# A state-space kernel's phase tables on GpSimd: two tables per instruction up to the last doubling

## The chip, the cores and the metric

One core of one Trainium2 chip runs the whole program. The metric is the device time of one execution in microseconds; lower is better. Inputs and outputs are float32.

## The reference

The program computes two stacked blocks on a sequence of 256 rows of width 1024. The first block has two layers (feed-forward, mixer, cross-attention to a memory of 256 rows, feed-forward); the mixer of the first layer is called even, that of the second odd. The second block has three parallel branches, one of which is a diagonal complex state-space recurrence with 2048 states, and a last feed-forward. What the change touches is the recurrence, cut to its core:

```python
ab_re, ab_im = mag * jnp.cos(li * dt), mag * jnp.sin(li * dt)      # one complex factor per state
x_re = jnp.einsum('bsgh,gph->bsgp', uf, bb_re)                     # inputs of the states
x_im = jnp.einsum('bsgh,gph->bsgp', uf, bb_im)
# h[t] = ab * h[t-1] + x[t], by an associative scan over the 256 rows
_, _, h_re, h_im = lax.associative_scan(combine, (a_re, a_im, x_re, x_im), axis=1)
y = einsum(h_re, c_re) - einsum(h_im, c_im) + d_skip * uf
```

## The kernel before

The kernel turns the input of the states by the angle of each row, scans with the real magnitude only, and turns the result back. For that it needs, for every state, the cosine and sine of the state's angle times 1 to 256. These are the phase tables: four tables J = 0 to 3 of 128 partitions by 2 (cosine, sine) by 4 blocks by 256 rows, 1 MB each.

They are built early, on GpSimd, while the first feed-forward runs, and written ("spilled") to DRAM, from where they are read back in the second block. `phase_table(J)` (L2728) waits for the angles of VectorE, copies the 8 first columns (L2736) and then doubles: from n columns it makes columns n to 2n, by a complex product with column n-1. Each doubling is two triples: two products into the scratch `K.tabs` (L2744, L2745; `vsb` in the trace) and their difference or sum into the table (L2747; `R` in the trace). `before()` makes GpSimd wait for its own last instruction ahead of L2744 and of L2747. Eight doublings of 4n = 4 to 512 elements a partition make a table. The DMA at L2750 spills it. Tables 0 and 2 are built in `K.qT`, tables 1 and 3 in `K.kT`, two neighbouring quarters of `R1`; so table J from 2 on waits for the spill of J-2. Next on GpSimd's queue is `decay_bias` (L2759), which waits for VectorE in the even mixer. ScalarE waits for spills 2 and 3 ahead of its first write to `qT` in the even mixer (L1327, L1328).

The other engines run their own programs in a fixed order written out by hand. All weights are float32 and are split into two parts for TensorE: SyncE's queue loads a piece into `raw` (five buffers), ScalarE rounds it to `whi` (L1118), VectorE computes the rest `wlo` (L1677), and TensorE multiplies with both (L445 to L447). There are three buffers of each part: ScalarE can round a piece when TensorE has finished the one three pieces before, and VectorE works two pieces ahead of TensorE. What else VectorE has to do stands between two L1677, in program order.

One such thing is `row_rstd` (from L1715 on), the reciprocal root of the mean square of the rows of a normalisation. It is a chain of small instructions, each waiting for the one before: L1726, L1729, L1731 and L1732 (these two don't depend on each other), L1734, and three times two L1738 and two L1742. In the first feed-forward it runs for the memory's rows, `row_rstd("m")`, after the sixth chunk of columns. At the start of the even and the odd mixer it runs for the rows of `x`; behind it L1747 (VectorE) and L1144 (ScalarE) write the normalised rows `O`, which TensorE transposes (L511). The lower part of the memory's transposed rows (`mT`, L1762) is computed in eight steps between the weight pieces of the tenth and eleventh chunk of the first feed-forward.

Of the kernel before, what the change touches and what calls it, by code (L numbers as in the profile page):

```python
# [10 lines left out]
ALU = mybir.AluOpType  # L11
ACT = mybir.ActivationFunctionType
AX = mybir.AxisListType.X
P = 128
# [102 lines left out]
class Kernel:  # L117
# [33 lines left out]
    def memory(self):  # L151
# [9 lines left out]
        R1 = self.R1 = sb("R1", [P, 8192])  # L161
# [38 lines left out]
        self.CL = [b.rearrange("p (j n) -> p j n", j=4) for b in self.sqj]  # L200
        self.early = [self.qT, self.kT]
        self.pq0 = [a.rearrange("p (r j) n -> p r j n", r=2) for a in self.early]
        self.pq = [self.M[:, i, :].rearrange("p (r j n) -> p r j n", r=2, j=2) for i in range(2)]
        self.spill = self.nc.dram_tensor("phases", (4, P, 2048), F32, kind="Internal").ap()
        self.cum = self.nc.dram_tensor("cum", (8, 256), F32, kind="Internal").ap()
# [8 lines left out]
        c = self.cst  # L214
# [119 lines left out]
BLOCKS = (0, 2, 1, 3)  # L334
# [2357 lines left out]
def pool_program(K, G, A):  # L2692

    S, E, D = K.S, K.nc.gpsimd, K.D
    pool = Engine(E)

    def before():

        pool.wait_ge(*S.pool_own.latest())
# [20 lines left out]
    def mem_load():  # L2720

        pool.wait_ge(*S.turned.at("squares"))
        for t in range(2):
            E.dma_start(K.O[:, t, :], D["mem"].rearrange("b (t p) d -> t p (b d)", p=P)[t]).then_inc(*S.mem.done(0, step=16))
        pool.wait_ge(*S.xlo.at(("h", "f0", 3, 1)))
        mem_turned(0)

    def phase_table(J):  # L2728

        tab = K.pq0[J % 2]  # L2730
        pool.wait_ge(*S.trig.at("phases"))
        if J >= 2:
            pool.wait_ge(*S.spilled[J - 2].at(0))
        for ri in range(2):
            for i, block in enumerate(BLOCKS):
                E.tensor_copy(tab[:, ri, i, 0:1], K.SM[:, 2 + ri, 4 * J + block:4 * J + block + 1]).then_inc(*S.pool_own.done())  # L2736
        n = 1
        while n < 256:
            c, s = tab[:, 0, :, 0:n], tab[:, 1, :, 0:n]
            cw, sw = (tab[:, i, :, n - 1:n].to_broadcast([P, 4, n]) for i in range(2))  # L2740
            u1, u2 = K.tabs[:, 0, :, 0:n], K.tabs[:, 1, :, 0:n]
            for out, (a, b), op in ((0, (cw, sw), ALU.subtract), (1, (sw, cw), ALU.add)):
                before()
                E.tensor_tensor(u1, c, a, ALU.mult).then_inc(*S.pool_own.done())  # L2744
                E.tensor_tensor(u2, s, b, ALU.mult).then_inc(*S.pool_own.done())  # L2745
                before()
                E.tensor_tensor(tab[:, out, :, n:2 * n], u1, u2, op).then_inc(*S.pool_own.done())  # L2747
            n *= 2
        before()
        E.dma_start(K.spill[J], K.early[J % 2].rearrange("p k t -> p (k t)")).then_inc(*S.spilled[J].done(0, step=16))  # L2750

    def load_table(q):

# [5 lines left out]
    def decay_bias():  # L2759

        pool.wait_ge(*S.scan.at("neg"))
        E.dma_start(K.cum, K.cumT[:, 1, :]).then_inc(*S.cum.done(0, step=16))
        pool.wait_ge(*S.cum.at(0))
        E.dma_start(K.biasA[:, :, :], bass.AP(K.cum.tensor, K.cum.offset, [[0, P], [256, 8], [1, 256]])).then_inc(*S.dec.done(0, step=16))
# [45 lines left out]
    small_loads()  # L2810
    pool.wait_ge(*S.loaded[0].at(20))
    mem_load()
    for J in range(4):
        phase_table(J)
    decay_bias()
    for t in range(2):
        decay_rows(t, range(4))
# [68 lines left out]
def build(nc, D, known):  # L2886

    with ExitStack() as ctx:
        K = Kernel(nc, D, ctx, known)
        G, A = gemms(K), attentions(K)  # L2890
        pe_program(K, G, A)
        act_program(K, G, A)
        dve_program(K, G, A)
        pool_program(K, G, A)
        sp_program(K, G, A)
        return K.known()
# [61 lines left out]
```

## Time and profile before

| | |
|---|---|
| median of 3 runs | 1626.81 us (1624.32 to 1627.3) |
| profiled execution, its own time | 1623.05 us |
| its span (first to last instruction) | 1621.8 us |
| granted TensorE clock | 0.999 |
| TensorE matmul busy | 1595.5 us (98%) |
| VectorE busy | 1109.3 us (68%) |
| ScalarE busy | 861.6 us (53%) |
| GpSimd busy | 227.5 us (14%) |

In the profile PE is TensorE (PEld its weight loads), DVE is VectorE, ACT is ScalarE, POOL is GpSimd and SPq is SyncE's DMA queue. A row of a timeline gives the start in us from the span's start, the length in us, the engine, the line of the kernel, the instruction with what it writes and reads, and in brackets how long the engine had been idle before it and for whom. Rows that follow each other with the same line are merged, with their count (x2). The length of an instruction counts what it waits inside the engine. Matmuls overlap, so a row of 0.39 us may start 0.23 us after the one before it.

### The profile page before, as it was taken

Reading aid. Unit: us, or ns where it says so; the run is one execution under the profiler, and the core shown is the slowest. Engines: PE = TensorE matmul, PEld = TensorE weight load, DVE = VectorE, ACT = ScalarE, POOL = GpSimd, SP = SyncE. Lnnn points to the kernel's source line nnn. Section 1 sums busy time; section 2 is a strip of 40 time slices with the busy share of each in tenths; the row PEclk is TensorE's granted clock in tenths of the full one; section 3 lists DMA queues with packets and bytes.
Section 4 is the critical chain, followed back from the end, with each engine's and each line's share of the span. In section 5 each row is a group of like instructions: output and inputs, shape, how many; then the busy total and the mean of one; then the engine's idle time right before and its main releaser. Section 6 shows DMA issues by size and latency. Waiting matters only on the chain.

```text
span 1621.8 us, 21203 instructions
## 1 busy us (share of the span) xinstructions
PE 1595.5 (98%) x8050; PEld 1331.2 (82%) x8050; DVE 1109.3 (68%) x1769; ACT 861.6 (53%) x1324; POOL 227.5 (14%) x351
## 2 busy tenths in 40 slices
PE   8999999999999999999999999999999999999998
PEld 6888877788888888888889888888889877888886
DVE  6775788867655556555596775655568997776566
ACT  5554556855545445444555555544454457454444
POOL 2499901000000000000000000000014442100000
PEclk9999999999999999999999999999999999999999
DMA  9766656445455565655654553555685554556563
GB/s 283 242 208 213 207 169 191 150 142 156 140 185 188 188 186 178 191 185 190 213 171 156 163 186 111 183 187 187 189 261 166 165 157 143 182 194 193 188 188 109
DMA packets 187543, 295.22 MB, mean 182 GB/s; under 512 B 13510, under 2 KB 108144, under 8 KB 186160
## 3 DMA queue, kind: packets, MB, share of 16 engines
q1 hardware_dynamic: 183264, 275.93, 54.4%
q0 software_dynamic: 3888, 17.60, 3.4%
q8 instruction: 64, 1.05, 0.3%
q10 hardware_dynamic: 288, 0.33, 0.1%
q14 instruction: 39, 0.32, 0.1%
HBM read 288.29 MB, written 5.25 MB: 181 GB/s over the span
## 4 chain that ended last, share of the span: by engine, by line
PE 86%; DVE 8%; ACT 3%; issue 2%; POOL 1%; DMA 0%; SPq 0%; DVEq 0%; ACTq 0%
PE b L445 25%; PE b L447 24%; PE b L446 24%; PE b L667 4%; DVE wlo L1677 2%; PE b L669 2%; ACT whi L1118 1%; PE b L690 1%; PE b L920 1%; PE b L902 1%; PE b L511 1%; PE b L527 1%; PE b L611 1%; PE b L564 1%; ACT R L1207 1%
## 5 line engine op out<-in xcount | busy, mean ns | idle before, releaser
L1677 DVE TENSOR_TENSOR wlo<-raw,whi 128x1024 fp32r<-128x1024 f32 (+1 forms) x523 | 648.7, 1243 | 430.6 <-ACT whi L1118 429.2
L1118 ACT ACTIVATE whi<-raw 128x1024 fp32r<-128x1024 f32 (+1 forms) x523 | 549.8, 1053 | 554.3 <-PE b L447 518.4
L445 PE MATMUL b<-whi,hT 128*128 128x512 f32 (+1 forms) x1040 | 413.0, 397 | 9.4 <-DVE wlo L1677 8.2
L447 PE MATMUL b<-whi,hT 128*128 128x512 f32 (+1 forms) x1040 | 404.8, 389 | 0.0
L446 PE MATMUL b<-wlo,hT 128*128 128x512 f32 (+1 forms) x1040 | 404.3, 389 | 0.0
L445 PE MATMUL b<-whi,oT 128*128 128x512 f32 x672 | 265.1, 394 | 0.0
L447 PE MATMUL b<-whi,oT 128*128 128x512 f32 x672 | 262.0, 390 | 0.0
L446 PE MATMUL b<-wlo,oT 128*128 128x512 f32 x672 | 261.6, 389 | 0.0
L445 PEld LDWEIGHTS b<-whi,hT 128*128 128x128 f32 x1040 | 195.8, 188 | 54.7 <-DVE wlo L1677 10.4
L447 PEld LDWEIGHTS b<-whi,hT 128*128 128x128 f32 x1040 | 195.7, 188 | 41.6
L446 PEld LDWEIGHTS b<-wlo,hT 128*128 128x128 f32 x1040 | 196.0, 188 | 37.7
L447 PEld LDWEIGHTS b<-whi,oT 128*128 128x128 f32 x672 | 126.1, 188 | 26.9
L445 PEld LDWEIGHTS b<-whi,oT 128*128 128x128 f32 x672 | 126.2, 188 | 26.2 <-DVE R L2501 0.5
L446 PEld LDWEIGHTS b<-wlo,oT 128*128 128x128 f32 x672 | 126.3, 188 | 25.3
L667 PE MATMUL b<-hT,whi 128*128 128x512 f32 x256 | 90.8, 399 | 0.0
L1207 ACT ACTIVATE R<-R,st 128x256 f32<-128x256 f32 (+1 forms) x96 | 43.5, 455 | 73.3 <-DVE st L1861 30.5
L669 PE MATMUL b<-hT,wlo 128*128 128x256 f32 x256 | 71.9, 281 | 0.0
L2822 POOL DMA_DIRECT2D biasB<-in_rel x1 | 0.5, 527 | 490.8 <-PE b L690 490.8
L1249 ACT ACTIVATE biasA<-b,st 128x256 f32<-128x256 f32 x88 | 41.1, 474 | 44.6 <-PE b L447 41.2
L445 PE MATMUL b<-hT,whi 128*128 128x256 f32 (+1 forms) x216 | 62.2, 288 | 0.1
L446 PE MATMUL b<-hT,whi 128*128 128x256 f32 (+1 forms) x216 | 61.1, 283 | 0.0
L447 PE MATMUL b<-hT,wlo 128*128 128x256 f32 (+1 forms) x216 | 61.0, 283 | 0.0
(349 smaller groups left out, 1855.9 us busy)
## 6 DMA issues: line engine op xcount, KB each, us to landing
raw<-in_ffn_w_in SPq DMA_DIRECT2D x350, 256.0 KB, 3.2
raw<-in_ffn_w_out SPq DMA_DIRECT2D x88, 512.0 KB, 3.4
raw<-in_w_ff SPq DMA_DIRECT2D x64, 512.0 KB, 4.0
raw<-in_w_in SPq DMA_DIRECT2D x36, 512.0 KB, 3.7
raw<-in_x_w_kv SPq DMA_DIRECT2D x32, 512.0 KB, 4.1
raw<-in_even_w_in SPq DMA_DIRECT2D x24, 512.0 KB, 4.2
raw<-in_odd_w_in SPq DMA_DIRECT2D x24, 512.0 KB, 4.0
raw<-in_x_w_q SPq DMA_DIRECT2D x16, 512.0 KB, 4.1
```

Source lines behind the costliest of these rows:

```text
L445: T.matmul(out, ah, bh, start=start, stop=False, skip_group_check=skip)
L446: T.matmul(out, ah, bl, start=False, stop=False, skip_group_check=skip)
L447: return T.matmul(out, al, bh, start=False, stop=stop, skip_group_check=skip)
L511: ins = T.transpose(banks[b][:, (2 * i + t) * P:(2 * i + t + 1) * P], src[:, t, kt * P:(kt + 1) * P], ident)
L527: ins = T.transpose(banks[b][:, i * P:(i + 1) * P], K.sqj[t][:, i * P:(i + 1) * P], ident)
L564: ins = T.transpose(banks[b][:, k * P:(k + 1) * P], src[:, k * P:(k + 1) * P], ident)
L667: T.matmul(bank[:, :].rearrange("p (a t) -> p a t", a=2), hi[:, kk, cs], K.hs[:, :, kt, :], start=kt == 0, stop=False, skip_group_check=True)
L669: ins = T.matmul(bank[:, 256:512], lo[:, kk, cs], K.hT[0][:, kt, :], start=False, stop=kt == 7, skip_group_check=True)
L1118: E.activation(K.whi[j % NSPLIT][:, 0:n], K.raw[j % NRAW][:, 0:n], ACT.Copy).then_inc(*S.whi.done(j))
L1207: ins = E.activation(s3[:, h, :], s3[:, h, :], ACT.Exp, bias=nm[:, h:h + 1], accum_out=sm[h])
L1249: E.activation(s[:, 0:256], bank[:, 0:256], ACT.Silu, scale=K.stat(("y", f.name), 2)[:, t:t + 1]).then_inc(*S.silu.done((f.name, c, t)))
L1677: V.tensor_tensor(K.wlo[j % NSPLIT][:, 0:n], K.raw[j % NRAW][:, 0:n], K.whi[j % NSPLIT][:, 0:n].bitcast(F32), ALU.subtract).then_inc(*S.wl ...
```

## The change

`phase_table(J)` becomes `phase_tables(first)`, which builds tables `first` and `first + 1`. A new view `K.pq01` covers `qT` and `kT` together, with the table as an extra dimension. The copies of the first columns are made for both tables (16 of them). For n = 1 to 64 one doubling with instructions of 8n elements a partition serves both tables, with the scratch split in two halves. For n = 128 the scratch holds one table only, so the two tables are doubled one after the other, each followed by its spill. The second call waits for the spills of both tables 0 and 1 before it starts. The arithmetic of each element is the same.

```diff
--- before.py
+++ after.py
@@ -200,6 +200,7 @@
         self.CL = [b.rearrange("p (j n) -> p j n", j=4) for b in self.sqj]
         self.early = [self.qT, self.kT]
         self.pq0 = [a.rearrange("p (r j) n -> p r j n", r=2) for a in self.early]
+        self.pq01 = R1[:, 4096:8192].rearrange("p (b r j n) -> p b r j n", b=2, r=2, j=4)
         self.pq = [self.M[:, i, :].rearrange("p (r j n) -> p r j n", r=2, j=2) for i in range(2)]
         self.spill = self.nc.dram_tensor("phases", (4, P, 2048), F32, kind="Internal").ap()
         self.cum = self.nc.dram_tensor("cum", (8, 256), F32, kind="Internal").ap()
@@ -2725,29 +2726,40 @@
         pool.wait_ge(*S.xlo.at(("h", "f0", 3, 1)))
         mem_turned(0)
 
-    def phase_table(J):
-
-        tab = K.pq0[J % 2]
+    def phase_tables(first):
+
         pool.wait_ge(*S.trig.at("phases"))
-        if J >= 2:
-            pool.wait_ge(*S.spilled[J - 2].at(0))
-        for ri in range(2):
-            for i, block in enumerate(BLOCKS):
-                E.tensor_copy(tab[:, ri, i, 0:1], K.SM[:, 2 + ri, 4 * J + block:4 * J + block + 1]).then_inc(*S.pool_own.done())
+        if first:
+            for J in range(first):
+                pool.wait_ge(*S.spilled[J].at(0))
+        for J in (first, first + 1):
+            for ri in range(2):
+                for i, block in enumerate(BLOCKS):
+                    E.tensor_copy(K.pq0[J % 2][:, ri, i, 0:1],
+                                  K.SM[:, 2 + ri, 4 * J + block:4 * J + block + 1]).then_inc(*S.pool_own.done())
         n = 1
         while n < 256:
-            c, s = tab[:, 0, :, 0:n], tab[:, 1, :, 0:n]
-            cw, sw = (tab[:, i, :, n - 1:n].to_broadcast([P, 4, n]) for i in range(2))
-            u1, u2 = K.tabs[:, 0, :, 0:n], K.tabs[:, 1, :, 0:n]
-            for out, (a, b), op in ((0, (cw, sw), ALU.subtract), (1, (sw, cw), ALU.add)):
-                before()
-                E.tensor_tensor(u1, c, a, ALU.mult).then_inc(*S.pool_own.done())
-                E.tensor_tensor(u2, s, b, ALU.mult).then_inc(*S.pool_own.done())
-                before()
-                E.tensor_tensor(tab[:, out, :, n:2 * n], u1, u2, op).then_inc(*S.pool_own.done())
+            if n < 128:
+                tables, both = [K.pq01], K.tabs.rearrange("p a j (b m) -> p a b j m", b=2)
+                parts = [tuple(both[:, a, :, :, 0:n] for a in range(2))]
+            else:
+                tables = [t.unsqueeze(1) for t in K.pq0]
+                parts = [tuple(K.tabs[:, a, :, 0:n].unsqueeze(1) for a in range(2))] * 2
+            for i, (tab, (u1, u2)) in enumerate(zip(tables, parts)):
+                b = len(K.pq0) // len(tables)
+                c, s = tab[:, :, 0, :, 0:n], tab[:, :, 1, :, 0:n]
+                cw, sw = (tab[:, :, r, :, n - 1:n].to_broadcast([P, b, 4, n]) for r in range(2))
+                for out, (x, y), op in ((0, (cw, sw), ALU.subtract), (1, (sw, cw), ALU.add)):
+                    before()
+                    E.tensor_tensor(u1, c, x, ALU.mult).then_inc(*S.pool_own.done())
+                    E.tensor_tensor(u2, s, y, ALU.mult).then_inc(*S.pool_own.done())
+                    before()
+                    E.tensor_tensor(tab[:, :, out, :, n:2 * n], u1, u2, op).then_inc(*S.pool_own.done())
+                if n == 128:
+                    J = first + i
+                    before()
+                    E.dma_start(K.spill[J], K.early[J % 2].rearrange("p k t -> p (k t)")).then_inc(*S.spilled[J].done(0, step=16))
             n *= 2
-        before()
-        E.dma_start(K.spill[J], K.early[J % 2].rearrange("p k t -> p (k t)")).then_inc(*S.spilled[J].done(0, step=16))
 
     def load_table(q):
 
@@ -2810,8 +2822,8 @@
     small_loads()
     pool.wait_ge(*S.loaded[0].at(20))
     mem_load()
-    for J in range(4):
-        phase_table(J)
+    phase_tables(0)
+    phase_tables(2)
     decay_bias()
     for t in range(2):
         decay_rows(t, range(4))
```

## Rows read from the trace of the kernel before

**Rows 1.** The page: busy time of each engine
```profile
PE 1595.5 (98%) x8050; PEld 1331.2 (82%) x8050; DVE 1109.3 (68%) x1769; ACT 861.6 (53%) x1324; POOL 227.5 (14%) x351
```

**Rows 2.** A stretch; columns: length, busy time (instructions) per engine, clock, DMA
```profile
80.00:120.00 40.00, 40.00 (x183) 33.11 (x181) 28.52 (x43) 20.41 (x31) 36.83 (x64) 1.00 0.67 210
```

**Rows 3.** Timeline of TensorE at the even mixer; columns: start, length, instruction, idle before
```profile
205.68 0.39 PE L447 MATMUL b<-whi,mT 128*128 128x512 f32 x1
208.29 1.38 PE L511 MATMUL b<-cst,O 128*128 128x128 f32 x8 [2.22 <-DVE O L1747]
...
214.01 0.48 PE L445 MATMUL b<-whi,hT 128*128 128x512 f32 x1
```

**Rows 4.** Timeline of TensorE at the odd mixer
```profile
815.58 0.39 PE L447 MATMUL b<-whi,mT 128*128 128x512 f32 x1
815.82 1.03 PE L511 MATMUL b<-cst,O 128*128 128x128 f32 x8
...
820.96 0.47 PE L445 MATMUL b<-whi,hT 128*128 128x512 f32 x1
```

**Rows 5.** Timeline of VectorE at the even mixer
```profile
201.91 1.01 DVE L1726 TENSOR_TENSOR st<-st 128x2 f32<-128x2 f32 x1
202.94 0.98 DVE L1729 TENSOR_SCALAR st<-st 128x2 f32<-128x2 f32 x1
203.96 0.17 DVE L1731 TENSOR_SCALAR st<-st 128x2 f32<-128x2 f32 x1
204.04 1.26 DVE L1732 TENSOR_SCALAR st<-st 128x2 int32<-128x2 int32 x1
...
207.48 0.75 DVE L1747 TENSOR_SCALAR O<-x,st 128x1024 f32<-128x1024 f32 x1
```

**Rows 6.** Timeline of VectorE at the odd mixer
```profile
811.61 0.15 DVE L1726 TENSOR_TENSOR st<-st 128x2 f32<-128x2 f32 x1
...
814.42 0.76 DVE L1747 TENSOR_SCALAR O<-x,st 128x1024 f32<-128x1024 f32 x1
```

**Rows 7.** Timeline of GpSimd, first and fourth table
```profile
61.99 1.22 POOL L2736 COPY R<-SM 128x1 f32<-128x1 f32 x8 [9.28 <-DVE SM L2083]
...
65.82 0.20 POOL L2744 TENSOR_TENSOR vsb<-R 128x8 f32<-128x8 f32 x1
...
88.19 1.04 POOL L2744 TENSOR_TENSOR vsb<-R 128x512 f32<-128x512 f32 x1
...
99.10 0.60 POOL L2750 DMA_DIRECT2D phases<-R  x1 [0.30 <-POOL R L2747]
...
175.71 0.20 POOL L2744 TENSOR_TENSOR vsb<-R 128x8 f32<-128x8 f32 x1
...
196.62 1.90 POOL L2744 TENSOR_TENSOR vsb<-R 128x512 f32<-128x512 f32 x1
...
200.98 1.91 POOL L2744 TENSOR_TENSOR vsb<-R 128x512 f32<-128x512 f32 x1
...
202.85 1.05 POOL L2745 TENSOR_TENSOR vsb<-R 128x512 f32<-128x512 f32 x1
203.98 1.29 POOL L2747 TENSOR_TENSOR R<-vsb 128x512 f32<-128x512 f32 x1
```

**Rows 8.** DMA issues between 60 and 210 us; columns: count, size, us to landing
```profile
phases<-R POOLq DMA_DIRECT2D x4, 1024.0 KB, 5.4
```

**Rows 9.** Timelines of VectorE and of TensorE at the memory's chain
```profile
107.59 0.18 DVE L1726 TENSOR_TENSOR st<-st 128x2 f32<-128x2 f32 x1
...
110.92 2.45 DVE L1677 TENSOR_TENSOR wlo<-raw,whi 128x1024 fp32r<-128x1024 f32 x2
...
113.72 0.39 PE L445 MATMUL b<-whi,hT 128*128 128x512 f32 x1
```

**Rows 10.** Timeline of VectorE at the memory's subtractions
```profile
160.71 1.26 DVE L1762 SCALAR_TENSOR_TENSOR mT<-M,gcol,mT 128x256 fp32r<-128x256 f32 x1
...
168.50 2.31 DVE L1677 TENSOR_TENSOR wlo<-raw,whi 128x1024 fp32r<-128x1024 f32 x1
```

## The prediction

> **What bounds the kernel now.** I read the page first, its busy times: TensorE is busy for 98% of the span, GpSimd for 14% [rows 1]. Next I read the stretches: from 80 to 120 us, in the middle of the tables, GpSimd is busy for 36.83 of 40 us and TensorE is never idle [rows 2]. So a shorter GpSimd is worth nothing by itself, and the tables can matter only through the few places where TensorE waits. TensorE's own timeline shows the wait: after the matmul at 205.68 it stands still for 2.22 us for the normalised row `O` of VectorE, and the first matmul of the even mixer starts at 214.01, 8.33 us after that last one [rows 3]. The odd mixer's boundary has the same sequence at 815.58 and 820.96, only 5.38 us, with no idle time before its first transposes [rows 4].
>
> The difference lies in a chain of 17 tiny VectorE instructions, `row_rstd`: L1726, L1729, L1731, L1732, L1734, then six L1738 and six L1742. At 201.91 it needs 5.57 us to reach L1747 [rows 5], at 811.61 only 2.81 us [rows 6]. Three of its instructions took 1.01, 0.98 and 1.26 us, where L1726 takes 0.15 us elsewhere [rows 5, 6]. Each ends within 0.04 us of the end of a GpSimd multiply or sum on 512 elements (202.89, 203.90 and 205.27) [rows 7]. After 205.27 GpSimd has no tensor instruction left, and the chain comes from there to L1747 at 207.48 unhindered [rows 5, 7]. So a VectorE instruction of this chain waits for the whole GpSimd tensor instruction that is running; that costs TensorE 2.95 us here (8.33 less 5.38) and is the only price I can find of the tables in the kernel before.
>
> **Part 1: fewer instructions.** For two tables together the doublings n = 1 to 64 are issued once on double width instead of twice. A doubling of the table with width 4n becomes one of width 8n, and the trace has all those widths but not the four-dimensional pattern. In the fourth table the doublings at widths 8 to 256 took from 175.71 to 196.62, 20.9 us; in the first from 65.82 to 88.19, 22.4 us [rows 7]. The doubling at width 512 took from 88.19 to its DMA issue at 99.10, less a wait of 0.3, 10.6 us; in the fourth from 196.62 to 205.27, 8.6 us [rows 7]. With a uniform 10 us for that one, a pair costs 2.6 us of copies, 21 us, three times 10 us and two DMA issues with their waits at 0.9: 55.4 us, against 72 us for two tables now (61.99 to 205.6, halved). The first run of 512-wide work is thereby three doublings, 18 instructions, some 30 us long, instead of four separate runs of 6. That is the part with consequences.
>
> **Part 2: the added wait.** The third and fourth tables now wait for the second spill also, issued just before; a spill lands in 5.4 us [rows 8]. Queued behind that wait is only table work; the next after it, `decay_bias`, waits for a product of the even mixer, which starts after 206 us. The spills leave GpSimd's queue as before (four of 1 MB), the first at about 108 us instead of 99.10, the last at about 177 instead of 205.6. ScalarE asks for the last two only in the even mixer. Cost on the path: zero, covered by the 28 us from 177 to the even mixer; without cover it would be 5.4 us.
>
> **When GpSimd is where.** The first multiply comes after 16 copies instead of 8 (1.22 us for 8 [rows 7]) and one hold-up behind a VectorE subtraction, so between 64.5 and 65.6 us, nearly where width 8 began before (65.82). The 512-wide run then begins at about 87.7 us. 10.6 us for n = 64 gives 98.3; 10 us for the first table's last doubling gives 108.3; its DMA issue ends at 109.2; the second table's last doubling ends between 116 and 118.5. Wait for the spill: 122.9. The second pair: 2.6 + 20.9 + 31 gives 177.5 us. That is 24 us before 201.9, so the chain at the even boundary runs free. **Gain: 2.9 us** (between 2.2, the one wait, and 2.95).
>
> **What is hit instead.** `row_rstd("m")` is the same chain of 17, for the memory rows; it starts at 107.59 us and stands on VectorE in front of the next weight subtraction, L1677 at 110.92 [rows 9]. Before, GpSimd was then at its narrowest widths, and the chain took 3.3 us. Afterwards it falls into the 512-wide run. TensorE first needs that weight piece for its matmul at 113.72 [rows 9]; L1677 lasts about 1.2 us and so was ready at 112.1, 1.6 us early. Any longer chain than 4.9 us makes TensorE wait, and nothing later gives that back, since TensorE is full. Walk: the chain starts at 107.6 to 108.3 and gets about five instructions through while GpSimd ends its sum and issues the DMA (to 109.2). Twelve are left against six GpSimd instructions: 1.04, 1.05 and 1.29 us [rows 7] and small gaps, 3.5 us a triple, 7.1 us in all. At 201.91 four chain instructions passed in three of GpSimd's [rows 5, 7], so eight pass by 116.3, and four more take 0.7 us: the chain ends at 116.3 to 117.0, L1677 at 117.5 to 118.2, and TensorE waits 3.8 to 4.5 us. **Loss: 4.0 us.** Its ends: 0 (the chain passes mostly between instructions, or the run lies elsewhere) and 7.9 (GpSimd's run ends only at 118.5 and eleven instructions are left: 118.5 + 1.9 + 1.2 less 113.72).
>
> The Trainium skill (SBUF — State Buffer, section Who interferes with whom) says that a VectorE instruction with two SBUF inputs contends with a GpSimd instruction that reads SBUF, and that the second to issue blocks until the first is finished. The trace agrees for L1726 and speaks against this change. Taken strictly, one chain instruction per GpSimd instruction, six are left at 116.3: the wait would be 4.8 us instead of 4.0 and the sum 0.8 us higher.
>
> **A smaller hit.** Eight subtractions of the memory (`mT`, L1762) follow from 160.71 us on, one beside each weight piece, so for some 23 us. Under GpSimd's 512-wide run of the third table they took up to 1.26 us and a weight subtraction beside them 2.31 us [rows 10], and TensorE still did not wait. In the new order four or five of them, not three, lie in such a run (147 to 177). 0.2 us, between 0 and 1.
>
> **Sum.** -2.9 + 4.0 + 0.2 = +1.3 us. The profiled execution has 1623.05 us with a span of 1621.8; it would become 1624.4, span 1623.1. The median of the runs shown is 1626.81, 3.8 us above that execution, so 1628.1 us. A difference under 0.2% (3.3 us) is about what a measurement of this kernel can't tell from no change.
>
> **The rivals.** (a) Forecast: one wait replaced by a somewhat larger one, +1.3 us; own range 1626 to 1630.5. Chance 0.50. (b) The memory chain slips through: less than 1.5 us of wait, because GpSimd is at a gap or several chain instructions pass at each boundary. For it: instructions of a pair do not depend on each other, and L1731 passed unharmed [rows 5]. Against it: the run is 30 us long and covers 107.6 us even if my times are 8 us off. Then -2.9 + 0.5: 1624.4 us. Chance 0.20. (c) Slower: GpSimd comes later to the second table's last doubling, so that the chain meets eight or nine 512-wide instructions, 6.5 us of wait, and the memory's subtractions cost 1 more: +4.6, 1631.4 us. The sum is the chain's length less 7.6 us, so it decides from a chain of 10.9 us on (3.3 us, 0.2%); the forecast has 8.9. For it: each L1677 holds GpSimd up by about 0.9 us (10.6 against 7.1 us per doubling). Chance 0.20. (d) The joint instructions don't shorten GpSimd: a double pattern costs what it replaces or more. If the tables end after 202 us, the even boundary keeps its 2.95 us and the memory chain is hit as well: +4, 1630.8 us. Against it: duration goes by the element count at every width in the trace. Chance 0.10.
>
> **The chances.** Faster by over 0.2% needs the full gain, no new wait and some luck: 0.10, mostly from (b). Slower by over 0.2%: most of (c) and (d) and the upper edge of (a), 0.27. Within: 0.63. Range: (b) below and (c) above, 1623.8 to 1631.8 us.
>
> **What would show it.** Right: no wait before L511 near 206 us (or 210, shifted); L1726 to L1734 at the even boundary 0.15 to 0.17 us each; GpSimd's last spill at about 177 us; the `row_rstd` chain near 108 us taking 8 to 10 us, and behind it the largest new TensorE wait of the kernel, matmul L445 for `wlo` L1677. Wrong: that wait absent or under 1.5 us (then b), or a 512-wide run outside 88 to 118 us; spills still near 200 us (then d); any other idle time of TensorE between 120 and 200 us beyond 1 us.

## The result, and the profile after

| | before | after |
|---|---|---|
| median | 1624.79 us (12 runs, 1622.57 to 1627.3) | 1627.36 us (12 runs, 1626.51 to 1629.39) |
| span of the profiled execution | 1621.8 us | 1625.2 us |
| GpSimd busy | 227.5 us, 351 instructions | 198.9 us, 267 instructions |
| VectorE busy | 1109.3 us | 1113.4 us |

The ratio is 1.0018, with a 95% interval of 1.0010 to 1.0026: the changed kernel is slower by 2.9 us (1.6 to 4.2). GpSimd works 28.6 us less, and that is worth nothing by itself; the time goes by two places where TensorE waits.

The first is new. TensorE's timeline of the kernel after, at the piece that was first needed at 113.72 us in [rows 9]:

```profile
113.71 0.39 PE L448 MATMUL b<-whi,hT 128*128 128x512 f32 x1
119.36 0.80 PE L446 MATMUL b<-whi,hT 128*128 128x512 f32 x1 [5.25 <-DVE wlo L1678]
119.95 0.63 PE L447 MATMUL b<-wlo,hT 128*128 128x512 f32 x1
...
122.61 0.39 PE L448 MATMUL b<-whi,hT 128*128 128x512 f32 x1
```

It stands still for 5.25 us for the weight piece. Then a matmul starts every 0.43 us instead of every 0.23. The stretches of the same kernel (length, busy times per engine with counts, granted clock, DMA share, GB/s) say why: the granted clock is at half of full speed after the wait, the lower of its two levels (1.2 GHz of 2.4), and full again from about 122.4 us on.

```profile
119.40:122.10 2.70, 2.70 (x7) 2.15 (x8) 2.70 (x3) 0.00 (x0) 0.00 (x0) 0.50 0.93 320
122.40:125.00 2.60, 2.60 (x13) 2.16 (x12) 0.13 (x1) 1.06 (x1) 2.08 (x17) 1.00 0.99 269
```

What held the piece up is VectorE's timeline, which answers [rows 9]:

```profile
108.39 1.25 DVE L1727 TENSOR_TENSOR st<-st 128x2 f32<-128x2 f32 x1
109.68 0.17 DVE L1730 TENSOR_SCALAR st<-st 128x2 f32<-128x2 f32 x1
...
109.96 0.16 DVE L1733 TENSOR_SCALAR st<-st 128x2 int32<-128x2 int32 x1
110.16 2.48 DVE L1735 TENSOR_SCALAR st<-st 128x2 int32<-128x2 int32 x1
112.67 1.44 DVE L1739 SCALAR_TENSOR_TENSOR st<-st 128x1 f32<-128x1 f32 x2
114.15 1.03 DVE L1743 SCALAR_TENSOR_TENSOR st<-st 128x1 f32<-128x1 f32 x2
...
116.27 1.24 DVE L1743 SCALAR_TENSOR_TENSOR st<-st 128x1 f32<-128x1 f32 x2
117.55 0.35 DVE L1739 SCALAR_TENSOR_TENSOR st<-st 128x1 f32<-128x1 f32 x2
...
118.08 2.35 DVE L1678 TENSOR_TENSOR wlo<-raw,whi 128x1024 fp32r<-128x1024 f32 x2
```

The chain `row_rstd("m")` (in the kernel after, each of these line numbers is one higher) takes 9.7 us from 108.39 to the next weight subtraction at 118.08; in [rows 9] it took 3.3. GpSimd's timeline at the same time, which answers [rows 7]:

```profile
88.42 1.04 POOL L2754 TENSOR_TENSOR vsb<-R 128x512 f32<-128x512 f32 x1
...
107.47 2.16 POOL L2757 TENSOR_TENSOR R<-vsb 128x512 f32<-128x512 f32 x1
109.92 0.60 POOL L2761 DMA_DIRECT2D phases<-R  x1 [0.30 <-POOL R L2757]
110.55 1.05 POOL L2754 TENSOR_TENSOR vsb<-R 128x512 f32<-128x512 f32 x1
111.55 1.05 POOL L2755 TENSOR_TENSOR vsb<-R 128x512 f32<-128x512 f32 x1
112.68 1.29 POOL L2757 TENSOR_TENSOR R<-vsb 128x512 f32<-128x512 f32 x1
114.04 1.05 POOL L2754 TENSOR_TENSOR vsb<-R 128x512 f32<-128x512 f32 x1
115.05 1.04 POOL L2755 TENSOR_TENSOR vsb<-R 128x512 f32<-128x512 f32 x1
116.17 1.26 POOL L2757 TENSOR_TENSOR R<-vsb 128x512 f32<-128x512 f32 x1
117.73 0.59 POOL L2761 DMA_DIRECT2D phases<-R  x1 [0.30 <-POOL R L2757]
122.83 1.95 POOL L2738 COPY R<-SM 128x1 f32<-128x1 f32 x16 [4.51 <-DMA phases<-R]
...
177.09 0.59 POOL L2761 DMA_DIRECT2D phases<-R  x1 [0.30 <-POOL R L2757]
```

The 512-wide run goes from 88.42 to 117.43 us. The chain's first instruction ends at 109.64 with the sum of 107.47; the next three pass while GpSimd waits 0.30 us and begins to issue its DMA; from 110.55 to 117.43 GpSimd runs six instructions, and each of the rows from L1735 to the second L1743 ends within 0.15 us of the end of one of them. L1735 ends at 112.64 and was thus passed by two; the independent instructions of a pair went together (the pair of 114.15 took 1.03 us). Nine instructions of the chain passed in the six, and the last four ran free.

The second place is the gain. TensorE's timeline at the even mixer, which answers [rows 3]:

```profile
212.76 0.39 PE L448 MATMUL b<-whi,mT 128*128 128x512 f32 x1
212.99 1.03 PE L512 MATMUL b<-cst,O 128*128 128x128 f32 x8
...
217.00 1.44 PE L512 MATMUL b<-cst,O 128*128 128x128 f32 x8 [0.21 <-DVE hT L1756]
218.19 0.48 PE L446 MATMUL b<-whi,hT 128*128 128x512 f32 x1
```

The wait of 2.22 us for `O` is gone; from the last matmul before it to the first of the even mixer it is 5.43 us (212.76 to 218.19) instead of 8.33. VectorE's chain there takes 2.81 us (L1727 at 208.85, L1748 at 211.66).

The books, from the trace: the piece comes 5.42 us later (119.36 less 113.72, less 0.22 by which the whole profile started later). Eight matmul intervals behind it take 3.25 us (119.36 to 122.61) instead of 1.8: 1.4 us. The even boundary gives back 2.9. Sum 3.9 us, from one profiled execution of each kernel; the span grew by 3.4 and the timed runs by 2.9.

### The profile page after: what moved, and what is told of

Same layout as the page of the kernel before. It is cut to its first block, busy times and chain, and to the rows that moved or that the text cites. A ratio compares the mean times of both kernels' runs of the same rounds, so it can differ in the third digit from the quotient of the medians.

```text
span 1625.2 us, 21120 instructions
## 1 busy us (share of the span) xinstructions
PE 1596.6 (98%) x8050; PEld 1332.1 (82%) x8050; DVE 1113.4 (69%) x1769; ACT 861.6 (53%) x1324; POOL 198.9 (12%) x267
## 3 DMA queue, kind: packets, MB, share of 16 engines
HBM read 288.29 MB, written 5.25 MB: 181 GB/s over the span
## 4 chain that ended last, share of the span: by engine, by line
PE 85%; DVE 8%; ACT 4%; issue 2%; POOL 1%; DMA 0%; SPq 0%; DVEq 0%; ACTq 0%
PE b L446 24%; PE b L448 24%; PE b L447 24%; PE b L668 4%; DVE wlo L1678 2%; PE b L670 2%; ACT whi L1119 1%; PE b L691 1%; PE b L921 1%; PE b L903 1%; PE b L512 1%; PE b L528 1%; PE b L612 1%; PE b L565 1%; ACT R L1208 1%
```

## The experiments

**Theory A**: a VectorE instruction of the chain waits until the GpSimd tensor instruction that runs is finished; the change costs or gains only by where GpSimd's 512-wide run lies against the two chains. **Theory B**: the joint instructions, or the wait for two spills, cost TensorE something by themselves. **Theory C**: the two engines share a bandwidth, and it is GpSimd's amount of work beside the chain that counts.

In the profiles the first 70 us differ by up to 2 us from one execution to the next. The column "marked" therefore gives the time from the small wait of TensorE near 73 us, which every kernel here has, to the second row of transposes at the even mixer (at 73.13 and 212.81 us in the kernel before: 139.7 us), less that of before. It comes from one execution of each kernel. Each ratio is to runs of the kernel before on the same occasion; "after, second pair held" has 5 runs, the others 10 to 12.

| kernel | ratio (95% interval) | timed, us | marked, us | wait at the memory's chain | wait for `O` | last spill issued |
|---|---|---|---|---|---|---|
| after | 1.0018 (1.0010 to 1.0026) | +2.9 | +4.0 | 5.25 | none | 177.1 |
| second pair only | 0.9989 (0.9980 to 0.9998) | -1.8 | -1.6 | none | none | 197.5 |
| after, chain later | 0.9988 (0.9979 to 0.9997) | -1.9 | -1.9 | none | none | 182.1 |
| before, chain later | 1.0017 (1.0008 to 1.0026) | +2.8 | +3.0 | 3.46 | none | 206.9 |
| after, second pair held | 1.0041 (1.0028 to 1.0053) | +6.7 | +7.3 | 5.25 | 1.09 | 212.6 |
| after, halves | 0.9994 (0.9985 to 1.0002) | -1.0 | -1.3 | 1.32 | none | 197.7 |
| after, all in narrow | 0.9979 (0.9970 to 0.9989) | -3.4 | -2.8 | none | none | 185.2 |

**Second pair only.** Tables 0 and 1 as before, 2 and 3 together.

```diff
-    phase_tables(0)
+    phase_table(0)
+    phase_table(1)
     phase_tables(2)
```

> Tables 0 and 1 are built one after the other as before, only tables 2 and 3 are built together. Theory A (a VectorE instruction of the chain row_rstd waits for the whole GpSimd tensor instruction that runs; what counts is where the 512-wide run lies): the memory's chain at about 108 us meets narrow instructions and takes 3.3 us, TensorE doesn't wait there; the tables end near 190 us, so the chain at the even mixer is free too. Against the kernel before: 2.9 us less (ratio 0.9982, span 1618.9). Theory B (the joint instructions on two tables, or the wait for two spills, cost TensorE something themselves): about half of the change's loss stays, ratio about 1.000 or above.

Theory B falls: the joint instructions and the wait for both spills are in this kernel, and it is faster than before. But it gained 1.8 us, not 2.9. TensorE's timeline of this kernel names the rest:

```profile
189.28 0.94 PE L691 MATMUL b<-cst,biasB 128*128 128x128 f32 x4 [0.77 <-DVE biasB L1953]
```

This is a new wait of 0.77 us behind the memory's eight subtractions, seven of which took 0.91 to 1.28 us (0.47 free).

**The changed kernel, chain later.**

```diff
-        {1: trig_rows, 5: lambda: row_rstd("m")})
+        {1: trig_rows, 6: lambda: row_rstd("m")})
```

> The changed kernel with row_rstd of the memory one chunk later on VectorE (about 125 us), where GpSimd waits for the second spill or is at its narrowest widths. Theory A: the wait of 5.25 us and the slow matmuls behind it vanish, the even mixer stays free; 2.9 us less than the kernel before (ratio 0.9982), some 5.5 to 6.5 us less than the changed one. Theory B: nothing changes against the changed kernel (ratio 1.0018).

VectorE's timeline of this kernel: the chain's first row, the weight subtraction behind it, and two of the memory's subtractions (L1763) with the weight subtraction between them:

```profile
124.97 0.15 DVE L1727 TENSOR_TENSOR st<-st 128x2 f32<-128x2 f32 x1
...
127.70 1.22 DVE L1678 TENSOR_TENSOR wlo<-raw,whi 128x1024 fp32r<-128x1024 f32 x1
...
168.55 1.27 DVE L1763 SCALAR_TENSOR_TENSOR mT<-M,gcol,mT 128x256 fp32r<-128x256 f32 x1
169.74 2.31 DVE L1678 TENSOR_TENSOR wlo<-raw,whi 128x1024 fp32r<-128x1024 f32 x1
171.97 1.25 DVE L1763 SCALAR_TENSOR_TENSOR mT<-M,gcol,mT 128x256 fp32r<-128x256 f32 x1
```

The chain takes 2.7 us (124.97 to 127.70), as free as in [rows 6]. With it the 5.25 us and the slow matmuls are gone: by the ratios, 0.9988 and 1.0018, 4.9 us less than the changed kernel (5.5 to 6.5 were expected), and 5.9 us less in the marked stretch. Six of the eight L1763 lie beside 512-wide instructions and last 0.9 to 1.3 us instead of 0.48, the weight pieces between them 2.1 to 2.3, and TensorE waits 0.71 us once, at 173.77. So here too 1.9 us came out where 2.9 were expected.

**The kernel before, chain later.** The same one-line edit without anything of the change.

> The kernel before, nothing changed on GpSimd, only row_rstd of the memory one chunk later (about 125 us), where GpSimd's second table is in its 512-wide doubling (123.8 to 134.3 us). Theory A: the chain takes 8 to 10 us there and TensorE waits 4 to 5 us, plus slow matmuls behind it if the wait is long; the even mixer keeps its 2.95 us; ratio 1.003 to 1.004. Theory B: no difference from the kernel before.

VectorE's timeline of this kernel at the memory's chain, then a row of TensorE and one of GpSimd:

```profile
126.69 0.99 DVE L1726 TENSOR_TENSOR st<-st 128x2 f32<-128x2 f32 x1
127.72 0.97 DVE L1729 TENSOR_SCALAR st<-st 128x2 f32<-128x2 f32 x1
...
130.30 1.90 DVE L1738 SCALAR_TENSOR_TENSOR st<-st 128x1 f32<-128x1 f32 x2
...
134.84 2.39 DVE L1677 TENSOR_TENSOR wlo<-raw,whi 128x1024 fp32r<-128x1024 f32 x2
```

```profile
136.15 0.79 PE L445 MATMUL b<-whi,hT 128*128 128x512 f32 x1 [3.46 <-DVE wlo L1677]
...
204.45 2.16 POOL L2747 TENSOR_TENSOR R<-vsb 128x512 f32<-128x512 f32 x1
```

The chain takes 8.2 us (126.69 to 134.84), TensorE waits 3.46 us (4 to 5 were expected), and its next matmuls start 0.43 us apart. So the damage needs nothing of the change, only the chain beside 512-wide work: the same edit helps the one kernel and harms the other. What was expected of the even mixer did not come: there is no wait for `O`, since the wait had moved the chain there to 209.62 us, and GpSimd's last table ended at 206.61. From the last matmul before the boundary to the first of the even mixer it is 5.95 us instead of 8.33, which is why the ratio is 1.0017 and not 1.003.

**The changed kernel, second pair held.**

```diff
             for J in range(first):
                 pool.wait_ge(*S.spilled[J].at(0))
+            pool.wait_ge(*S.wlo.at(51))
```

> The changed kernel, but GpSimd starts tables 2 and 3 only when weight piece 51 has been split (157.6 us instead of 122.8), so that they end at about 211.5 us, inside the even mixer's chain (208.9 to 211.4 us). Theory A: the gain of the change is lost again, 2 to 3 us more than the changed kernel, ratio to before about 1.0035, with L1727 to L1735 at the even mixer at about 1 us each and TensorE waiting about 2 us ahead of its first transposes. If instead the 35 us of slack on GpSimd were all that counts (nobody reads the tables until the second block), no difference from the changed kernel: 1.0018.

VectorE's timeline at the even mixer in this kernel, then a row of GpSimd and one of TensorE:

```profile
211.06 1.24 DVE L1727 TENSOR_TENSOR st<-st 128x2 f32<-128x2 f32 x1
212.33 0.17 DVE L1730 TENSOR_SCALAR st<-st 128x2 f32<-128x2 f32 x1
...
214.95 0.75 DVE L1748 TENSOR_SCALAR O<-x,st 128x1024 f32<-128x1024 f32 x1
```

```profile
210.13 2.15 POOL L2758 TENSOR_TENSOR R<-vsb 128x512 f32<-128x512 f32 x1
...
215.76 1.38 PE L512 MATMUL b<-cst,O 128*128 128x128 f32 x8 [1.09 <-DVE O L1748]
```

A part of the gain is lost again: 1.09 us of wait for `O` (about 2 were expected), and 3.7 us more than the changed kernel by the ratios, 3.4 in the marked stretch. Only one instruction of the chain, L1727, met a GpSimd instruction (the last, ending at 212.28), so the others were not slowed, against what was expected; but the chain also began 2.2 us later than in the changed kernel. Of the 3.4 us, 1.6 are the wait and what follows it at the boundary (the first transposes last 1.38 instead of 1.03 us, the second wait is 0.36 instead of 0.21); 0.5 lie at 194.66, at a wait of 0.18 us and slower transposes behind the memory's subtractions; and 0.9 have nothing to do with the boundary: the matmuls behind the 5.25 us stayed slow for longer than in the changed kernel. The remaining 0.4 I can't place. So what belongs to the even boundary is 1.6 of the 2.9 us; this kernel supports the gain term less strongly than its 3.7 us look.

**Halves.** Every 512-wide instruction becomes two of 256 elements.

```diff
-            if n < 128:
+            if n < 64:
...
+                w = 4 if n < 128 else 2
+                parts = [(t.unsqueeze(1)[:, :, :, j:j + w, :], *(K.tabs[:, a, j:j + w, 0:n].unsqueeze(1) for a in range(2)))
+                         for t in K.pq0 for j in range(0, 4, w)]
```

> The changed kernel with every GpSimd instruction of 512 elements replaced by two of 256 (n = 64 one table at a time, n = 128 two blocks of four at a time); same arithmetic, more instructions. If VectorE waits for the end of one whole GpSimd instruction (theory A), the memory's chain is let in twice as often: it takes 6 to 7 us instead of 9.7, TensorE waits 2 to 3 us instead of 5.25, and if the wait stays as short as the 2.22 us at the even mixer in the kernel before, no slow matmuls follow: ratio 0.9995 to 1.000. If instead the two engines share a bandwidth (theory C), the chain is slowed by the same total work of GpSimd: 9 to 10 us, wait about 5 us, ratio 1.0018 or above.

VectorE and then GpSimd and TensorE in this kernel, at the memory's chain:

```profile
107.67 0.70 DVE L1727 TENSOR_TENSOR st<-st 128x2 f32<-128x2 f32 x1
...
109.67 0.89 DVE L1739 SCALAR_TENSOR_TENSOR st<-st 128x1 f32<-128x1 f32 x2
110.60 0.60 DVE L1743 SCALAR_TENSOR_TENSOR st<-st 128x1 f32<-128x1 f32 x2
...
114.03 2.77 DVE L1678 TENSOR_TENSOR wlo<-raw,whi 128x1024 fp32r<-128x1024 f32 x2
```

```profile
110.50 0.62 POOL L2755 TENSOR_TENSOR vsb<-R 128x256 f32<-128x256 f32 x1
111.07 0.62 POOL L2756 TENSOR_TENSOR vsb<-R 128x256 f32<-128x256 f32 x1
111.77 0.74 POOL L2758 TENSOR_TENSOR R<-vsb 128x256 f32<-128x256 f32 x1
...
115.29 0.50 PE L446 MATMUL b<-whi,hT 128*128 128x512 f32 x1 [1.32 <-DVE wlo L1678]
```

The chain takes 6.4 us instead of 9.7, though GpSimd is busy beside it nearly throughout and issues more instructions for the same work. That speaks against a shared bandwidth (C) and for a wait to the end of one instruction: what counts is how long a single GpSimd instruction is. TensorE waited only 1.32 us, less than the 2 to 3 expected; 0.7 us of that is that the chain began earlier than in the changed kernel (107.67, not 108.39). No slow matmul followed. The ratio's interval, 0.9985 to 1.0002, includes no change; it is below that of the changed kernel.

**All in narrow.** The chain one chunk later, and the subtractions of the memory two chunks earlier on ScalarE and VectorE.

```diff
-                  **{(9 + k // 4, k % 4): mem_halves(0, k) for k in range(8)}}, {4: mem_squares})
+                  **{(7 + k // 4, k % 4): mem_halves(0, k) for k in range(8)}}, {4: mem_squares})
...
-                  **{(9 + k // 4, k % 4): mem_lows(0, k) for k in range(8)}},
-        {1: trig_rows, 5: lambda: row_rstd("m")})
+                  **{(7 + k // 4, k % 4): mem_lows(0, k) for k in range(8)}},
+        {1: trig_rows, 6: lambda: row_rstd("m")})
```

> The changed kernel with the memory's row_rstd one chunk later (as in e2) and the eight subtractions of the memory, with ScalarE's halves of them, two chunks earlier (about 127 to 150 us instead of 161 to 184), where GpSimd is at its narrow widths for tables 2 and 3. Theory A: no wait of TensorE from 80 us to the even mixer, the 0.7 us of e2 gone too; 2.9 us less than before, ratio 0.9982. If the 0.7 us was not from the subtractions under 512-wide instructions: as e2, 0.9988.

TensorE is never idle from 80 to 206 us:

```profile
80.00:206.00 126.00, 126.00 (x573) 1.00 0.69 217
```

This version is faster than both kernels: ratio 0.9979 (0.9970 to 0.9989) to the kernel before, 3.4 us; in the marked stretch 2.8. Against the changed kernel with only the chain later (-1.9 in that stretch) 0.9 us more is gained, and the wait of 0.71 us behind the memory's subtractions is gone, as expected. The intervals of the two ratios overlap, so this last step rests on the trace.

## Why the prediction was right, and where it was off

The forecast was a difference of +1.3 us with a 50% chance, one wait replaced by a larger one. Measured are +2.9 us by the runs and +3.4 by the spans. 1627.36 us lies in the range and in the forecast's own range, 0.7 us below the 1628.1 forecast. That closeness is partly luck: the forecast started from a median of three runs, 1626.81 us, which is 2.0 us above the median of twelve, and its difference was 1.3 us too small by the medians; the two errors offset each other. The prediction also took a difference under 0.2% as not to be told from none; the measured 0.18% has an interval of 0.10 to 0.26% and is told from none. The mechanism was the one forecast, but for the clock; the terms measured:

- **Where GpSimd is.** Forecast: the run from 87.7, first spill's issue done at 109.2, end of the run 116 to 118.5, last spill at about 177.5. Trace: 88.42, 110.52, 117.43, 177.09. A doubling of width 8n cost on the joint pattern what it costs on a single table, so rival (d) is out.
- **The gain of 2.9 us.** It was 2.9 (8.33 less 5.43). The held kernel shows the other side: with the tables ending inside the chain, the wait for `O` is back.
- **The loss of 4.0 us.** This term was mis-sized: it was 6.8, of which 5.4 is the wait and 1.4 the slow matmuls. For the wait, the chain's part was right: it began at 108.39 (forecast 107.6 to 108.3), then nine instructions passed in GpSimd's last six (forecast eight) and four ran free. What came later was GpSimd: its 512-wide run began 0.7 us later (88.42 instead of 87.7), and its first two doublings took 21.2 us instead of 20.6 (to 109.63). So its last six began at 110.55 instead of 109.2 and ended at 117.43 instead of 116.3, and the chain with them. The slow matmuls were in no term: I had taken a wait of TensorE to cost its own length. That is the step that was missing; added to the forecast's sum, its 1.4 us make +2.7. The strict form of the rule, by which only six would have passed (the Trainium skill, SBUF — State Buffer, Who interferes with whom), fits the dependent instructions here, of which at most one passed per GpSimd instruction, but the two of a pair went through together.
- **The memory's subtractions, 0.2 us.** In the changed kernel it was nothing: the stall had pushed them back so far that only three lay under the run, as before. Without the stall, in the two kernels that avoid the chain, the wait behind them was 0.7 to 0.8 us, and their marked stretches are 0.9 to 1.2 us longer than that of the last kernel (-1.9 and -1.6 against -2.8). That is at the upper bound of 1 or a little above it: this term was too small for a kernel without the stall.
- **The added wait.** GpSimd stood 4.5 us for the second spill, forecast 5.4, and nothing waited for it. That it costs nothing is also what the second pair alone shows; it was not taken away by itself, since the buffers would be overwritten.

Rival (c), slower with a wait of 6.5 us and 1 us of subtractions, is as near in size as the forecast by the timed runs (+2.9 lies 1.6 above +1.3 and 1.7 below +4.6), and nearer by the spans (+3.4). It gets there by a mixture: a shorter wait than it had, and slow matmuls that it didn't have. Rival (b) is refuted by the timeline. The measured 0.18% falls within 0.2%, which had 0.63, close to its edge.

## What to carry to other kernels

Before making an engine off the critical path faster or its instructions longer, list what the engines that it can hold up do at that time. Here a chain of small dependent VectorE instructions paid up to one whole GpSimd instruction per link: 17 instructions that take 2.8 us free took 9.7 beside instructions of 1.0 to 1.3 us. Place such chains, and what else stands in front of a weight piece, beside short instructions of the other engine or none; here moving two steps by one and two chunks turned a loss of 0.18% into a gain of 0.21%. And look at the granted clock behind every stall of TensorE before pricing it.

## What the runs showed of the hardware that I had not expected

**The clock after a short stall.** After 5.25 and 3.46 us without a matmul the granted clock was at its lower level (0.50 and 0.52 of full in the stretch after), for six to ten matmuls about 0.43 us apart. The longest stretch was in the held kernel, after the same 5.25 us: it cost 2.3 us more than at full clock, where the changed kernel's cost 1.4. In the kernel before with the late chain it cost 1.7. After 2.22 us (kernel before, [rows 3]), 1.32 us and 0.8 us the granted clock stayed at 1.00. The stretch of the kernel before with the late chain:

```profile
136.00:139.30 3.30, 3.15 (x7) 0.52 0.94 300
```

So a wait of that length cost a quarter to a half more than itself. The Trainium skill (TensorE: Matmul & The Clock Gate, Part 1) names these two levels and that an idle TensorE falls to the lower one; these rows agree.

**Being passed twice.** L1735 at 110.16 took 2.48 us and ended with the second of two GpSimd instructions; in the kernel before with the late chain, no single instruction took more than 1.27 us (a pair, at 130.30, took 1.90). It was issued while GpSimd issued a DMA, but in the held kernel L1733 and L1735 ran beside such an issue at 0.16 and 0.17 us. In the kernel with halves a pair that began beside such an issue (L1743 at 113.01) took 1.09 us. Why L1735 lost twice stays open.
